# Reordered router and first unit in a fused block of mLSTM, differential attention and grouped experts

## The reference, cut to what matters

```python
h = layer_norm(DN_ALPHA * h + merged @ w_out[l], ln1_g[l], ln1_b[l])
ffn = group_moe(h, w_router, router_bias, w_gate_e[l], w_up_e[l], w_down_e[l])
h = layer_norm(DN_ALPHA * h + ffn, ln2_g[l], ln2_b[l])

# group_moe: 16 experts in 4 groups of 4, top_k = 2
probs = softmax(xt @ w_router)
sel = probs + router_bias
top_group = argmax(max of sel in each group)
idx = top_k(where(in_group, sel, NEG), 2)
w = take(probs, idx); w = w / sum(w)
for e in range(16):
    y += combine[:, e] * ((silu(xt @ w_gate[e]) * (xt @ w_up[e])) @ w_down[e])
```

## Time and profile before

| | |
|---|---|
| median of 3 runs | 779.58 us |
| lowest and highest | 778.72, 779.71 us |
| profiled execution, span from first to last instruction | 777.8 us |
| profiled execution, own time | not given apart from the span; the median lies 1.8 us above the span |
| instructions | 12443 |
| PE busy | 744.4 us (96%) |
| DVE busy | 344.5 us (44%) |
| ACT busy | 253.7 us (33%) |
| mean granted clock of TensorE | 0.988 |
| DMA | 251.42 MB, 323 GB/s over the span |
| output projection ends, first gather, first gate product | 326.9, 335.8, 341.7 us |

### The profile page before, as it was taken

The page is one execution under the profiler, slowest core; times in us unless marked ns, Lnnn a source line. Parts: engine busy times, 40 slices in busy tenths (PEclk is TensorE's granted clock), DMA queues, the critical chain, the costliest instruction groups (busy, mean ns, idle before and its releaser), DMA issues.

```text
span 777.8 us, 12443 instructions
## 1 busy us (share of the span) xinstructions
PE 744.4 (96%) x4408; PEld 453.7 (58%) x4409; DVE 344.5 (44%) x857; ACT 253.7 (33%) x537; POOL 27.8 (4%) x56
## 2 busy tenths in 40 slices
PE   8999999999999999989999999999999998898894
PEld 6978789997889999843333333333333332332341
DVE  7687566535768777574213221222213211211205
ACT  5665434547667555421111101111111101101111
POOL 3032000000001000000000000000000000000000
PEclk9999999999999999999999999999999999999997
DMA  9795414335050875989999999999999999999994
GB/s 279 309 349 217 172 46 166 138 132 214 2 213 5 323 297 233 430 321 393 420 428 428 424 428 427 429 423 432 428 421 433 428 421 431 428 421 430 425 423 162
DMA packets 39075, 251.42 MB, mean 323 GB/s; under 512 B 6177, under 2 KB 13426, under 8 KB 24194
## 3 DMA queue, kind: packets, MB, share of 16 engines
q1 hardware_dynamic: 38896, 250.93, 78.9%
q10 hardware_dynamic: 146, 0.04, 0.0%
HBM read 249.91 MB, written 1.05 MB: 323 GB/s over the span
## 4 chain that ended last, share of the span: by engine, by line
PE 69%; SPq 17%; DVE 6%; DMA 5%; issue 2%; ACT 1%; POOL 0%; DVEq 0%; ACTq 0%; POOLq 0%
PE ps L2236 26%; PE ps L1823 8%; PE ps L1825 8%; PE ps L1824 8%; DMA down_x<-in_w_down_e_dram 5%; SPq L604 4%; PE ps L2183 3%; SPq L623 2%; SPq L589 2%; PE ps L1900 2%; PE ps L2190 1%; PE ps L2171 1%; SPq L601 1%; DVE xc L1216 1%; SPq L616 1%
## 5 line engine op out<-in xcount | busy, mean ns | idle before, releaser
L2236 PE MATMUL ps<-raw,xg 128*64 128x512 f32 x512 | 117.0, 608 | 9.1 <-DMA raw<-in_w_gate_e_dram 6.1
L1823 PE MATMUL ps<-hi_h,whi 128*128 128x272 f32 (+1 forms) x384 | 111.7, 291 | 0.4 <-DVE wlo L1133 0.3
L1825 PE MATMUL ps<-hi_h,wlo 128*128 128x272 f32 (+1 forms) x384 | 109.5, 285 | 0.0
L1824 PE MATMUL ps<-lo_h,whi 128*128 128x272 f32 (+1 forms) x384 | 109.2, 284 | 0.0
L1133 DVE TENSOR_TENSOR wlo<-raw,whi 128x512 fp32r<-128x512 f32 x128 | 82.6, 687 | 37.9 <-ACT whi L765 37.3
L2236 PEld LDWEIGHTS ps<-raw,xg 128*64 128x64 f32 x512 | 37.9, 140 | 85.4 <-issue 76.3
L765 ACT CAST whi<-raw 128x512 fp32r<-128x512 f32 (+1 forms) x128 | 74.1, 618 | 14.7 <-PE ps L1825 12.3
L1823 PEld LDWEIGHTS ps<-hi_h,whi 128*128 128x128 f32 x384 | 72.4, 189 | 4.3 <-issue 2.5
L1825 PEld LDWEIGHTS ps<-hi_h,wlo 128*128 128x128 f32 x384 | 72.5, 189 | 0.0
L1824 PEld LDWEIGHTS ps<-lo_h,whi 128*128 128x128 f32 x384 | 72.4, 189 | 0.0
L2236 PE MATMUL ps<-gate_x,xg 128*64 128x512 f32 x256 | 56.9, 594 | 6.5 <-DMA gate_x<-in_w_gate_e_dram 6.5
(11 more groups left out here) (365 smaller groups left out, 1174.0 us busy)
## 6 DMA issues: line engine op xcount, KB each, us to landing
raw<-in_w_down_e_dram SPq DMA_DIRECT2D x16, 2048.0 KB, 32.9
gate_x<-in_w_gate_e_dram SPq DMA_DIRECT2D x15, 2048.0 KB, 32.0
raw<-in_w_in_dram SPq DMA_DIRECT2D x28, 1024.0 KB, 9.2
raw<-in_w_gate_e_dram SPq DMA_DIRECT2D x14, 2048.0 KB, 35.7
raw<-in_w_up_e_dram SPq DMA_DIRECT2D x14, 2048.0 KB, 37.1
down_x<-in_w_down_e_dram SPq DMA_DIRECT2D x8, 2048.0 KB, 35.7
up_x_right<-in_w_up_e_dram SPq DMA_DIRECT2D x16, 1024.0 KB, 36.2
up_x_left<-in_w_up_e_dram SPq DMA_DIRECT2D x8, 2048.0 KB, 36.3
```

What stands on the lines that cost most here:

```text
L1823: mm(o, w1, hi[:, k, c0:c0 + n], start=(k == 0), stop=False)
L1824: mm(o, w1, lo[:, k, c0:c0 + n], start=False, stop=False)
L1825: last = mm(o, w2, hi[:, k, c0:c0 + n], start=False, stop=(k == KB - 1))
L2236: last = mm(ps[r0:r0 + SLOTS, bank_no, :], lhs[:, k % 4, k // 4, :], w[:, k % 2, 512 * c:512 * c + 512], start=(k == 0), stop=(k == KB - 1))
```

## The change

In the output projection, `turn_part(1)` moves ahead of the last piece. In the last piece the loop goes tile by tile, and tile 0 is released in its middle (`tile0_out`), so that DVE adds its residual part there. Tile 1's last two column blocks are turned into another PSUM bank (`turned_late`), and ACT copies the last two column blocks per tile. The partial logits are copied and summed per tile, each with a release of its own, and one `clear` moves behind them. `sel` is compared as exponent plus bias times sum instead of exponent times reciprocal plus bias, which orders the experts alike. Half of the gain rows' spread into bank 2 moves from ahead of the ranks to between ranks and gather. For the first unit, `xg` is made by one multiply and one add per half instead of four operations. The expert and block of unit 1 come from two comparisons (`second`), and the tables are made behind `add_base(0)`; the picks of unit 1 come ahead of the base. PE reads one register instead of two before the first unit.

```diff
@@ -262,6 +262,7 @@
     unit_f = at("unit_f", [1, 2, UNITS], TABLES + 1408)
+    second = at("second", [1, 2, 1], TABLES + 1632, I32)
@@ -278,6 +279,8 @@
+    turned_late = ps[:, 5, 0:2 * P].rearrange("p (b c) -> p b c", c=P)
@@ -374,6 +377,7 @@
     s.rout_done = nc.alloc_semaphore("rout_done")
+    s.tile0_out = nc.alloc_semaphore("tile0_out")
@@ -725,7 +729,7 @@
         pool.wait_ge(s.resid_done, 2 * TT)
-        pool.wait_ge(s.logit_done, 1)
+        pool.wait_ge(s.logit_done, TT)
@@ -1024,12 +1028,16 @@
         act.activation(table_load[:], neglam[0:1, :], ACT.Exp)
-        for b in range(4):
+        for b in range(3):
...
-        act.wait_ge(s.ht_t1, 5)
-        act.copy(logit_parts[:], ps[:, 0, 0:T]).then_inc(s.ht_ready, 1)
+        for t, late_part in enumerate((turned1[:, KB - 2:KB, 0:P], turned_late)):
+            act.wait_ge(s.ht_t1, 4 + t)
+            act.copy(ht[:, KB - 2:KB, P * t:P * t + P], late_part).then_inc(s.ht_ready, 1)
...
+        act.wait_ge(s.ht_t1, 6)
+        for t in range(TT):
+            act.copy(logit_parts[:, P * t:P * t + P], ps[:, 0, P * t:P * t + P]).then_inc(s.ht_ready, 1)
@@ -1544,8 +1552,11 @@
         for part, used in ((1, 12), (2, PIECES)):
-            dve.wait_ge(s.pieces_used, OUT_BASE + used + NBUF)
+            if part == 1:
+                dve.wait_ge(s.pieces_used, OUT_BASE + used + NBUF)
             for t in range(TT):
+                if part == 2:
+                    dve.wait_ge(*((s.pieces_used, OUT_BASE + PIECES + NBUF) if t else (s.tile0_out, 1)))
@@ -1571,9 +1582,9 @@
-        def load_unit(u):
-            return (dve.value_load(unit_of[0:1, 0, bass.ds(u, 1)], min_val=0, max_val=NE - 1),
-                    dve.value_load(unit_of[0:1, 1, bass.ds(u, 1)], min_val=0, max_val=MAXBLK - 1))
+        def load_unit(u, table):
+            return (dve.value_load(table[0:1, 0, bass.ds(u, 1)], min_val=0, max_val=NE - 1),
+                    dve.value_load(table[0:1, 1, bass.ds(u, 1)], min_val=0, max_val=MAXBLK - 1))
@@ -1599,7 +1610,13 @@
             for c in range(2):
-                for a in range(4):
+                if first:
+                    half = xg[:, :, c, :]
+                    own(dve.tensor_tensor(half, turned_x[:, :, c, :], gain4[:, c, :].unsqueeze(2).to_broadcast([P, 4, SLOTS]),
+                                          ALU.mult))
+                    own.settle()
+                    last = dve.tensor_tensor(half, half, bias4[:, c, :].unsqueeze(2).to_broadcast([P, 4, SLOTS]), ALU.add)
+                for a in range(0 if first else 4):
@@ -1609,19 +1626,17 @@
                                  op1=ALU.mult).then_inc(s.nmr_ready, 1)
-        dve.wait_ge(s.logit_done, 1)
         for t in range(TT):
+            dve.wait_ge(s.logit_done, t + 1)
...
-        own(dve.reciprocal(rt[:, 15, 8:8 + TT], rt[:, 15, 4:4 + TT]))
-        own.settle()
         for t in range(TT):
-            own(dve.scalar_tensor_tensor(out=rt[:, 3, NE * t:NE * t + NE], in0=rt[:, 1, NE * t:NE * t + NE],
-                                         scalar=rt[:, 15, 8 + t:9 + t], in1=rbias[:], op0=ALU.mult, op1=ALU.add))
+            own(dve.scalar_tensor_tensor(out=rt[:, 3, NE * t:NE * t + NE], in0=rbias[:], scalar=rt[:, 15, 4 + t:5 + t],
+                                         in1=rt[:, 1, NE * t:NE * t + NE], op0=ALU.mult, op1=ALU.add))
@@ -1684,25 +1699,13 @@
         own(dve.tensor_copy(total[:], ends_f[:, src, 32 + NE - 1:32 + NE]))
+        for i, op in enumerate((ALU.is_lt, ALU.is_ge)):
+            own(dve.tensor_scalar(second[:, i, :], nblk_f[:, 0:1], 2.0, None, op))
...
         take_gathered(True)
-        every = unitno[:].unsqueeze(2).to_broadcast([1, UNITS, NE])
-        own(dve.tensor_tensor(passed[:], every, ends_f[:, src, 32:].unsqueeze(1).to_broadcast([1, UNITS, NE]), ALU.is_ge))
-        own.settle()
-        own(dve.tensor_reduce(unit_f[:, 0, :], passed[:], AX.X, ALU.add))
-        own.settle()
-        own(dve.tensor_tensor(passed[:], passed[:], nblk_f[:].unsqueeze(1).to_broadcast([1, UNITS, NE]), ALU.mult))
-        own.settle()
-        own(dve.tensor_reduce(unit_f[:, 1, :], passed[:], AX.X, ALU.add))
-        own.settle()
-        own(dve.tensor_tensor(unit_f[:, 1, :], unitno[:], unit_f[:, 1, :], ALU.subtract))
-        own(dve.tensor_scalar(unit_of[:, 0, :], unit_f[:, 0, :], float(NE - 1), None, ALU.min))
-        own.settle()
-        own(dve.tensor_scalar(unit_of[:, 1, :], unit_f[:, 1, :], float(MAXBLK - 1), None, ALU.min))
-        own.settle()
@@ -1719,19 +1722,37 @@
-        dve.wait_ge(s.h1_ready, TT)
-        dve.wait_ge(s.rows_b, 2)
-        scaled_norm(1)
-        e1, b1 = load_unit(1)
+        def unit_tables():
...
+            every = unitno[:].unsqueeze(2).to_broadcast([1, UNITS, NE])
+            own(dve.tensor_tensor(passed[:], every, ends_f[:, src, 32:].unsqueeze(1).to_broadcast([1, UNITS, NE]), ALU.is_ge))
+            own.settle()
+            own(dve.tensor_reduce(unit_f[:, 0, :], passed[:], AX.X, ALU.add))
+            own.settle()
+            own(dve.tensor_tensor(passed[:], passed[:], nblk_f[:].unsqueeze(1).to_broadcast([1, UNITS, NE]), ALU.mult))
+            own.settle()
+            own(dve.tensor_reduce(unit_f[:, 1, :], passed[:], AX.X, ALU.add))
+            own.settle()
+            own(dve.tensor_tensor(unit_f[:, 1, :], unitno[:], unit_f[:, 1, :], ALU.subtract))
+            own(dve.tensor_scalar(unit_of[:, 0, :], unit_f[:, 0, :], float(NE - 1), None, ALU.min))
+            own.settle()
+            own(dve.tensor_scalar(unit_of[:, 1, :], unit_f[:, 1, :], float(MAXBLK - 1), None, ALU.min))
+            own.settle()
...
+        e1, b1 = load_unit(0, second)
...
         pick_tokens(e1, b1)
+        dve.wait_ge(s.h1_ready, TT)
+        dve.wait_ge(s.rows_b, 2)
+        scaled_norm(1)
...
         dve.wait_ge(s.acc_base, 2 * TT)
+        unit_tables()
@@ -1752,7 +1773,7 @@
             weigh(e1)
-            e2, b2 = load_unit(u + 2)
+            e2, b2 = load_unit(u + 2, unit_of)
@@ -2081,13 +2102,14 @@
                 for k in range(c0 // P, (c0 + n) // P):
-                    last = pe.transpose(turned1[:, k, P * t:P * t + P], h1[:, t, P * k:P * k + P], ident[:])
-                    if t == TT - 1 and k % 2:
+                    to = turned1[:, k, P * t:P * t + P] if part < 2 or t == 0 else turned_late[:, k - (KB - 2), :]
+                    last = pe.transpose(to, h1[:, t, P * k:P * k + P], ident[:])
+                    if (part == 2 or t == TT - 1) and k % 2:
...
-            pe.wait_ge(s.ht_ready, 2 * half + 2)
+            pe.wait_ge(s.ht_ready, 3 * half + 2)
@@ -2107,36 +2129,40 @@
             pe.wait_ge(s.lo_ready, OUT_BASE + n + 1)
-            for i, k in enumerate(ks):
+            steps = [(i, t) for i in range(len(ks)) for t in range(TT)]
+            if n == PIECES - 1:
+                steps = [(i, t) for t in range(TT) for i in range(len(ks))]
+            for i, t in steps:
+                k = ks[i]
                 w1, w2 = (w[:, n % NBUF, width_n * i:width_n * i + width_n] for w in (whi, wlo))
-                for t in range(TT):
-                    o = out_bank(part, t)
-                    c = slice(P * t, P * t + P)
-                    mm(o, mg_hi[:, k, c], w1, start=(k == 0), stop=False)
-                    mm(o, mg_lo[:, k, c], w1, start=False, stop=False)
-                    last = mm(o, mg_hi[:, k, c], w2, start=False, stop=(k == KB - 1))
+                o = out_bank(part, t)
+                c = slice(P * t, P * t + P)
+                mm(o, mg_hi[:, k, c], w1, start=(k == 0), stop=False)
+                mm(o, mg_lo[:, k, c], w1, start=False, stop=False)
+                last = mm(o, mg_hi[:, k, c], w2, start=False, stop=(k == KB - 1))
+                if n == PIECES - 1 and (i, t) == (1, 0):
+                    last.then_inc(s.tile0_out, 1)
...
                 turn_part(0)
+                turn_part(1)
...
-        turn_part(1)
...
         logits(1).then_inc(s.ht_t1, 1)
-        for c in range(2):
-            clear(B_ACC[2 + c], True)
-        pe.wait_ge(s.ht_ready, 5)
+        clear(B_ACC[2], True)
         for t in range(TT):
-            last = mm(ps[:, 1 + 2 * t, 0:P].rearrange("p (r e) -> p r e", e=NE), logit_parts[:, P * t:P * t + P],
-                      group_sum[:].unsqueeze(1).to_broadcast([P, P // NE, NE]), start=True, stop=True)
-        last.then_inc(s.logit_done, 1)
+            pe.wait_ge(s.ht_ready, 6 + t)
+            mm(ps[:, 1 + 2 * t, 0:P].rearrange("p (r e) -> p r e", e=NE), logit_parts[:, P * t:P * t + P],
+               group_sum[:].unsqueeze(1).to_broadcast([P, P // NE, NE]), start=True, stop=True).then_inc(s.logit_done, 1)
+        clear(B_ACC[3], True)
@@ -2149,7 +2175,7 @@
             spread(C_L1B, range(4 * c, 4 * c + 4), B_ACC[c], True)
-        spread(C_L1G, range(4), 2)
+        spread(C_L1G, (0, 1), 2)
@@ -2159,6 +2185,7 @@
         mm(ps[:, 0, 2 * NE:3 * NE], ones_b, mask_b[:, 1, :], start=False, stop=True, **g).then_inc(s.rank_done, 1)
```

(4 more changed lines are left out.)

## The result

The changed kernel took 775.34 us (median of 4 runs, 775.01 to 775.68) where the kernel before took 779.34 (778.72 to 779.71): 4.0 us less, ratio 0.9949 with a 95% interval of 0.9933 to 0.9965. The profiled execution had a span of 773.6 us at a time of 775.38, so 1.8 us lie around the span. For the kernel before the forecast took 1.8 us too. Some 0.3 us of the gain therefore lie outside the span, where the forecast had nothing; why is open.

The account below looks back on a forecast made before the run. The prediction took the expert load stream's start and early fill as the bound, not PE's time per unit. Start 2.27 us earlier plus 0.5 won back made 2.8 us: span 775.0, plus 1.8, 776.8 us, range 775.5 to 778.4.

Parts of the forecast that it names:

- (a) to (c): Last output piece and turns, partial logits by tile, no reciprocal: 0.15, 0.30 and 0.20 us, 0.65 us at the first pick.
- (d): Norm rows between ranks and gather: PE's clock held at the gather, 1.4 us back (bounds 0 and 1.45).
- The rival: Clock falls anyway near the gather, or fell in the profiled execution but not typically: 778.2 us, chance 0.17.
- (e): First unit's xg by half in two operations instead of four: gain 0.22 us (bounds 0 and 0.3).
- (f): Tables made later: no stall at the up product, which comes 1.3 us earlier beyond the gate product's 2.27.
- the prediction's 5.3 us: Time on DVE from the end of xg to base_made in the new order, putting base_made at 346.1 us.
- the cover of 1.9 us: Slack before the up product: base_made forecast at 346.1 us, wanted by the up product at 348.0.
- the step that says how much the earlier up and down loads win back: Load stream behind its start: sooner up and down loads win back 0.5 us of 3.3 lost (bounds 0 and 1.3).
- more comes back than taken: Up and down loads decide, so the whole 2.27 + 1.3 us is seen: 776.0 us, chance 0.15.
- The rival of lower rates by mixed quarters: Quarters from two matrices in flight at once lower the DMA rate, 356 GB/s for 45 us: 781.5 us, chance 0.04.
- nothing arrives: Stream's end is set later by waits for free buffers, the start made up on the way: 779.5 us, chance 0.07.

Follow-up runs that it names:

- tables alone: Kernel before with only the unit tables moved behind the base and unit 1's picks put first: 776.76 us, ratio 0.9976.
- tables first: Changed kernel with the unit tables again ahead of the base and unit 1's picks behind the base's first part, two samples: 777.75 and 777.42 us.
- first row split: Changed kernel with expert 2's down weights fetched by quarters and its first gate quarter split, first row block released earlier: 775.62 us, ratio 0.9961.
- rows alone: Kernel before with only two column blocks of the gain rows moved between ranks and gather: 779.04 us, ratio 1.0002.
- down load late: Changed kernel with the first half of expert 2's down weights issued one quarter of the down product later: 776.89 us, ratio 0.9972.

## Why the prediction was right and wrong, by its steps

(a) to (c), 0.65 us: right. Tile 1's residual at 327.23, the first router step's pair ends at 330.62 in place of 331.10, `sel` starts at 331.60 in place of 332.28, the gather stands 0.69 us earlier.

(d) In the profiles right: from the gather to xg took 3.40 us in place of 4.71, which is 1.3 back of the 1.4. As a term of the median it was mis-sized: the moved rows are worth 0.3 us by the medians and nothing by the ratio, with room for 0.8. The profile of before showed a fallen clock, and the median was reckoned from that one span (plus 1.8) without asking how often the clock falls. The rival had this case with 0.17. The section of the Trainium skill that the prediction set against it ("TensorE: Matmul & The Clock Gate", "Why this matters for your kernels") asks for a longer idle gap; two profiles of the kernel before contradict that, and tables alone, with the same work of PE there and the clock at 1.00, shows that the gaps alone don't decide it.

(e) 0.22: right to 0.02, the first half of xg took 338.52 to 339.40, 0.88 us. PE's register read stayed under it.

(f) No stall at the up product: right. base_made came at 346.98 and not at 346.1. DVE stood 1.14 us for the two register reads ahead of unit 1's picks. In the kernel before these reads ran beside a base pair of 1.29 us and left only 0.27 us open, which is all that the prediction's 5.3 us held of them; in the new order only one add of 0.42 us runs beside them. Of the cover of 1.9 us, 1.1 stayed.

The sum is where it failed: the step that says how much the earlier up and down loads win back of the 3.3 us lost behind the start of the stream. "Bounds 0 and 1.3 us; I take 0.5, nearer to 0 because the share of DMA was already 0.97 in the poorest stretch": the term measured 1.4 us in bytes by 390 us (3.6 less the 2.2 of the start), above its own upper bound, and 1.7 to 2.6 us by the runs with the tables first. The share was the wrong column. In the earlier trace rows it reads 0.97 beside 356 GB/s and 1.01 beside 427, and with the first row split 1.01 stands beside 333: the share doesn't tell a full stream from a short one, GB/s does. (The Trainium skill, "Perfetto Trace Analysis", "Identifying the Most-Contended Engine", says to judge DMA by the bandwidth used and not by occupancy; this trace agrees, with 356 GB/s at 0.97.) The stretches from 344.5 to 375 lost 3.3 us before; with up and down loads 3.5 us earlier they lose 30.5 x (1 - 416/427) = 0.8.

Which load counts? Where all three move as the kernel's order moves them, the lead equals that of the down load: 3.5 for 3.6 (the change), 1.3 for 1.3 (rows alone), 2.6 for 2.6 (tables alone), 2.1 for 2.2 (tables first). But the down load doesn't decide alone. With up and down kept and gate 1.7 us late the lead loses 0.9; with gate and up kept and down 1.7 us late it loses 1.5; with down 1.7 us early it gains nothing. Each load counts as far as it finds the stream short. The rival "more comes back than taken" named this, with 776.0 us and 0.15. The rival of lower rates by mixed quarters is refuted: 431 GB/s in 355 to 360. That nothing arrives is refuted too: the lead is 3.6 us by 390 us and 3.8 behind 750.

The 776.8 came as near as it did by luck, because errors cancelled: 1.1 us or more too much for the clock, 0.9 (in bytes) to some 2 us (in the runs) too little for the up and down loads, and the 0.3 us outside the span, which no step had.

Open is up to 1 us at the end. The last load lands earlier or later than the bytes say, by amounts that differ between executions (755.33 and 756.90 us with the tables first, at leads of 2.3 and 2.0 behind 750 us), and the medians with the tables first lie 1.7 to 2.6 us above the changed kernel's for 1.4 of lead, an excess that the intervals don't hold apart from nothing. A stream made to run short otherwise (down load late) didn't show it in the median. What it is, no run here settles. Open is also which part of the new order pays: tables and picks of unit 1 were only moved together.

## What to carry to other kernels

Where a stream of loads sets the end, look at GB/s in short stretches behind its start, and treat every stretch below the steady rate as time to be won, whatever the DMA share reads. Then ask which requests found the stream short: here the first gate load and the first down load, held back by 1.7 us each, cost 0.9 and 1.5 us. The lead that such requests make lasted to the end, and the order of a few small operations on a side engine set when up's and down's came. A request that finds the stream full gains nothing by coming earlier. And before a fallen clock in one profile becomes a term of the sum, ask how often it falls: one profile is one execution.

## What the runs showed of the hardware

The same work of PE around the ranks (0.53 to 0.55 of 2.3 us busy) ran into a granted clock of 0.50 and 0.53 in two profiles (336.5 to 339.9 us) and 1.00 in a third. In one execution the clock also fell between 12 and 20 us (0.57 granted), behind 3.3 us in which PE had been busy for 2.45; with 2.68 in the same 3.3 us (9.4 to 12.7) the changed kernel held it. The fall put the turns 3.1 us later. DMA read a share of 0.97 at 356 GB/s and 1.01 at 333 and at 427. In 344.5 to 350 us the restarted stream ran at 357 GB/s, and at 333 with its first piece asked for 0.6 us sooner. Two register reads on DVE left 1.14 us before its next operation beside an add of 0.42 us, and 0.27 beside two operations of 1.29 us together. From 390 to 750 us the lead stayed within 0.2 us in the three profiles looked at (3.6 and 3.8; 2.2 and 2.3; 2.1 and 2.0), and the last landing strayed from the lead by up to 1.2 us.
